# Scores of the forgetting attention as three fp32r products with stacked high and low parts

## What is computed

```python
q = heads(q_in) * (dh ** -0.5)
k, v = heads(k_in), heads(v_in)
logf = jax.nn.log_sigmoid(f_pre.astype(f32)).transpose(0, 2, 1)
F = jnp.cumsum(logf, axis=-1)
...
    s = jnp.einsum('bhtd,bhsd->bhts', qb, k) + (fb[..., None] - F[:, :, None, :])
    s = jnp.where(pb[:, None] >= pos[None, :], s, -jnp.inf)
    p = jax.nn.softmax(s, axis=-1)
    return jnp.einsum('bhts,bhsd->bhtd', p, v)
```

## Time and profile before

| | us |
|---|---|
| median of three runs | 872.34 |
| lowest, highest | 872.18, 875.2 |
| the profiled execution | 872.08 |
| its span, first to last instruction | 870.3 |
| mean granted TensorE clock, share of full speed | 0.995 |
| input projection with the mixers in it, about | 38 to 399 |

### The profile page before, as it was taken

One profiled execution on the slowest core, in us unless ns is written; L12 is line 12 of the kernel. 1 busy time (PEld: TensorE's weight loads), 2 busy tenths in 40 slices (PEclk: granted clock), 3 DMA queues, 4 the chain that ended last, 5 costly groups with the idle time before them and its releaser, 6 DMA issues.

```text
span 870.3 us, 10546 instructions
## 1 busy us (share of the span) xinstructions
PE 847.0 (97%) x3932; PEld 681.4 (78%) x3932; DVE 438.8 (50%) x703; ACT 323.8 (37%) x478; POOL 48.2 (6%) x75
## 2 busy tenths in 40 slices
PE   5999999999999999999999999999999999999996
PEld 3578888877787777787888778888888888888886
DVE  6789877247778654225873453333333333323222
ACT  4535445442323444343333553333333332222231
POOL 5310000000000000000001110000000000000110
PEclk9899999999999999999999999999999999999999
DMA  9833223348775121114234223333333333333322
GB/s 357 264 77 104 72 73 90 79 145 289 253 256 170 49 73 49 49 49 169 74 97 121 73 73 96 96 96 96 96 96 96 96 96 91 105 96 90 103 72 96
DMA packets 149372, 100.67 MB, mean 116 GB/s; under 512 B 11072, under 2 KB 142552, under 8 KB 148312
## 3 DMA queue, kind: packets, MB, share of 16 engines
q1 hardware_dynamic: 149128, 100.14, 37.9%
q10 hardware_dynamic: 208, 0.05, 0.0%
HBM read 97.03 MB, written 2.10 MB: 114 GB/s over the span
## 4 chain that ended last, share of the span: by engine, by line
PE 87%; DVE 5%; DMA 3%; ACT 2%; issue 1%; SPq 1%; DVEq 0%; ACTq 0%
PE bank L1696 25%; PE bank L1698 25%; PE bank L1697 25%; DMA raw<-in_w_in 3%; PE bank L1913 2%; PE bank L1843 1%; PE bank L1935 1%; PE bank L1863 1%; PE bank L1874 1%; DVE wlo L1190 1%; PE bank L1960 1%; ACT whi L696 1%; PE bank L1926 1%; PE bank L1911 1%; PE bank L1815 0%
## 5 line engine op out<-in xcount | busy, mean ns | idle before, releaser
L1696 PE MATMUL bank<-h_lo,whi 128*128 128x512 f32 x712 | 285.9, 402 | 1.8 <-DVE wlo L1190 1.0
L1698 PE MATMUL bank<-h_hi,wlo 128*128 128x512 f32 x712 | 278.1, 391 | 0.0
L1697 PE MATMUL bank<-h_hi,whi 128*128 128x512 f32 x712 | 277.9, 390 | 0.0
L1696 PEld LDWEIGHTS bank<-h_lo,whi 128*128 128x128 f32 x712 | 134.2, 189 | 32.2 <-issue 3.7
L1697 PEld LDWEIGHTS bank<-h_hi,whi 128*128 128x128 f32 x712 | 134.3, 189 | 28.7 <-issue 1.7
L1698 PEld LDWEIGHTS bank<-h_hi,wlo 128*128 128x128 f32 x712 | 134.1, 188 | 28.8
L1190 DVE TENSOR_TENSOR wlo<-raw,whi 128x1024 fp32r<-128x1024 f32 x60 | 73.3, 1223 | 104.7 <-ACT whi L696 104.7
L696 ACT ACTIVATE whi<-raw 128x1024 fp32r<-128x1024 f32 x60 | 63.2, 1055 | 151.3 <-PE bank L1698 107.8
L1698 PE MATMUL bank<-a_hi,wlo 128*128 128x512 f32 x176 | 68.5, 389 | 0.0
L1696 PE MATMUL bank<-a_lo,whi 128*128 128x512 f32 x176 | 68.5, 389 | 0.0
L1697 PE MATMUL bank<-a_hi,whi 128*128 128x512 f32 x176 | 68.5, 389 | 0.0
(11 more groups left out here) (334 smaller groups left out, 1005.8 us busy)
## 6 DMA issues: line engine op xcount, KB each, us to landing
raw<-in_ffn_w SPq DMA_DIRECT2D x60, 512.0 KB, 3.8
raw<-in_w_in SPq DMA_DIRECT2D x44, 512.0 KB, 4.0
slab<-in_mod_w SPq DMA_DIRECT2D x32, 512.0 KB, 5.9
modA<-in_mod_w SPq DMA_DIRECT2D x4, 1024.0 KB, 10.9
modB<-in_mod_w SPq DMA_DIRECT2D x4, 1024.0 KB, 18.4
raw<-in_w_out SPq DMA_DIRECT2D x8, 512.0 KB, 3.7
raw<-in_ffn_w SPq DMA_DIRECT2D x8, 384.0 KB, 3.2
xtok<-in_x SPq DMA_DIRECT2D x4, 512.0 KB, 5.6
```

The costliest lines, as they stand in the source:

```text
L1696: mm(dst, w_h, m_l, start=first, stop=False)
L1697: mm(dst, w_h, m_h, start=False, stop=False)
L1698: return mm(dst, w_l, m_h, start=False, stop=last)
```

## The change

- fq chunks: one activation brings 128 rows into vtmp; ACT copies the two heads' halves into qst as fp32r (q high), and DVE subtracts them into the other half of the same head's 128 rows (fox_q_lo): a head's qst has q high in its own 64 rows and q low in the other 64.
- fk chunks: kf stays. ACT copies it in bodies 30 to 32 into khi, where each head has 128 rows with k high twice (four copies of 64 rows a chunk, fox_k_hi); DVE subtracts to klo, which lies on kf, in place (two a chunk, fox_k_lo).
- fox_scores: three fp32r products: the forget rows with nft and sel widened by zeros to 128 rows; qst by khi over 128 rows; qst's own 64 rows by klo. The product of the low parts is left out.
- POOL's clearing of qpad goes, w_glu is loaded in SP's step 22 behind a wait for the conv's output in place of the start, and hm, ym_lo, yf_hi, fox, mt1 and wglu have other addresses.

```diff
-        hm = at("hm", [P, 3, L], F32, 119)
+        khi = [at("khi0", [P, 3, L], F32R, 119), at("khi1", [P, 3, L], F32R, 131)]
...
-        qpad = at("qpad", [P, FH, L], F32, Z + 18.125)
+        qst = at("qst", [P, FH, L], F32R, Z + 18.125)
         kf = at("kf", [P, 3, L], F32, Z + 30.125)
+        klo = at("klo", [P, 3, L], F32R, Z + 30.125)
...
+                if s == 22:
+                    sp_.wait_ge(s_cx, 3)
+                    sp_.dma_start(wglu[:], w_glu.rearrange("(k p) n -> p k n", p=P)).then_inc(s_wglu, 16)
...
                 elif kind == "fq":
-                    act.wait_ge(s_pad, 3)
-                    A(qpad[0:FD, 2 * i, :], src[0:FD, :], ACT.Identity, bias=bq8[0:FD, i:i + 1],
-                      scale=FD ** -0.5)
-                    A(qpad[FD:P, 2 * i + 1, :], src[FD:P, :], ACT.Identity,
-                      bias=bq8[FD:P, i:i + 1], scale=FD ** -0.5).then_inc(s_evac, 1)
+                    act.wait_ge(s_vt, 6)
+                    if i == 2:
+                        act.wait_ge(s_qlo, 1)
+                    q = vtmp[:, i % 2]
+                    A(q, src[:], ACT.Identity, bias=bq8[:, i:i + 1], scale=FD ** -0.5).then_inc(s_evac, 1)
+                    act.wait_ge(s_evac, s + 1)
+                    A(qst[0:FD, 2 * i], q[0:FD], ACT.Copy)
+                    A(qst[FD:P, 2 * i + 1], q[FD:P], ACT.Copy).then_inc(s_qhi, 1)
...
+            def fox_k_hi(i):
+
+                act.wait_ge(s_mqk, MH)
+                act.wait_ge(s_evac, A_CHUNKS.index(("fk", i)) + 1)
+                even, odd = (khi[h // 3][:, h % 3] for h in (2 * i, 2 * i + 1))
+                A(even[0:FD], kf[0:FD, i], ACT.Copy)
+                A(odd[FD:P], kf[FD:P, i], ACT.Copy)
+                A(even[FD:P], kf[0:FD, i], ACT.Copy)
+                A(odd[0:FD], kf[FD:P, i], ACT.Copy).then_inc(s_khi, 1)
...
+                if 30 <= t < 33:
+                    fox_k_hi(t - 30)
...
+            def fox_q_lo(i):
+
+                dve.wait_ge(s_qhi, i + 1)
+                q = vtmp[:, i % 2]
+                V.tensor_tensor(qst[FD:P, 2 * i], q[0:FD], qst[0:FD, 2 * i].bitcast(F32), ALU.subtract)
+                V.tensor_tensor(qst[0:FD, 2 * i + 1], q[FD:P], qst[FD:P, 2 * i + 1].bitcast(F32),
+                                ALU.subtract).then_inc(s_qlo, 1)
+
+            def fox_k_lo(i):
+
+                dve.wait_ge(s_khi, i + 1)
+                even, odd = (khi[h // 3][:, h % 3] for h in (2 * i, 2 * i + 1))
+                V.tensor_tensor(klo[0:FD, i], kf[0:FD, i], even[0:FD].bitcast(F32), ALU.subtract)
+                V.tensor_tensor(klo[FD:P, i], kf[FD:P, i], odd[FD:P].bitcast(F32), ALU.subtract).then_inc(s_klo, 1)
...
+                if 19 <= t < 22:
+                    fox_q_lo(t - 19)
+                if 30 <= t < 33:
+                    fox_k_lo(t - 30)
...
                     pe.wait_ge(s_mp, NT * MH)
-                    pe.wait_ge(s_evac, A_CHUNKS.index(("fk", 2)) + 1)
+                    pe.wait_ge(s_qlo, 3)
+                if t == 0:
+                    pe.wait_ge(s_klo, h // 2 + 1)
                 b = ps[3 + n % 2][:, 0:ln]
-                mm(b, sel[0:42, MH + h:MH + h + 1].broadcast_to([42, P]), nft[:, t % 2, 0:ln],
+                mm(b, sel[:, MH + h:MH + h + 1].broadcast_to([P, P]), nft[:, t % 2, 0:ln],
                    start=True, stop=False)
-                mm(b, qpad[:, h, t * P:(t + 1) * P], kf[:, h // 2, 0:ln], start=False,
-                   stop=True).then_inc(s_fs, 1)
+                own, q = slice(FD * (h % 2), FD * (h % 2) + FD), qst[:, h, t * P:(t + 1) * P]
+                mm(b, q, khi[h // 3][:, h % 3, 0:ln], start=False, stop=False)
+                mm(b, q[own], klo[own, h // 2, 0:ln], start=False, stop=True).then_inc(s_fs, 1)
```

More of the change, by code:

```diff
@@ L179, in build @@
         wqk = at("wqk", [P, 12, MD], F32, X)
-        wglu = at("wglu", [P, 2, S5W], F32, X + 4.5)
+        wglu = at("wglu", [P, 2, S5W], F32, X + 11.5)
         pm = at("pm", [P, 1280], F32, X + 6.5)
@@ L195, in build @@
         msq = at("msq", [P, NT, MW], F32, Z)
+        hm = at("hm", [P, 3, L], F32, Z)
         mo = at("mo", [P, 3, L], F32, Z + 6.125)
         vf = at("vf", [P, NT, FW], F32, Z + 12.125)
-        qpad = at("qpad", [P, FH, L], F32, Z + 18.125)
+        qst = at("qst", [P, FH, L], F32R, Z + 18.125)
         kf = at("kf", [P, 3, L], F32, Z + 30.125)
+        klo = at("klo", [P, 3, L], F32R, Z + 30.125)
         fz = at("fz", [36, L], F32, Z + 30.125)
@@ L209, in build @@
         bbar = at("bbar", [P, 2, NS5, GD], F32, Z + 39.125)
-        nft = at("nft", [42, 2, L], F32R, Z + 40.125)
+        nft = at("nft", [P, 2, L], F32R, Z + 40.125)
         negr = at("negr", [36, L], F32R, Z + 42.125)
@@ L220, in build @@
         assert Z + 46.125 <= 207.5
-        fox = at("fox", [P, 3, L], F32, X)
-        ym_lo = at("ym_lo", [P, 3, L], F32R, X + 6)
+        fox = at("fox", [P, 3, L], F32, X + 6)
+        ym_lo = at("ym_lo", [P, 3, L], F32R, Z)
         ys_hi = at("ys_hi", [P, 2, L], F32R, X + 13.5)
         ys_lo = at("ys_lo", [P, 2, L], F32R, X + 17.5)
-        yf_hi = at("yf_hi", [P, 3, L], F32R, Z)
+        yf_hi = at("yf_hi", [P, 3, L], F32R, X)
         yf_lo = at("yf_lo", [P, 3, L], F32R, Z + 6)
@@ L233, in build @@
         xT = at("xT", [P, KB, L], F32, XT + 16)
-        mt = [at("mt0", [P, 3, L], F32, 115), at("mt1", [P, 3, L], F32, X)]
+        mt = [at("mt0", [P, 3, L], F32, 115), at("mt1", [P, 3, L], F32, X + 6)]
         sq = at("sq", [P, 2, L], F32, 115)
@@ L292, in build @@
         s_evac = sem("w_in_chunk_out")
+        s_wglu = sem("w_glu_loaded")
+        s_qhi = sem("fox_q_hi")
+        s_qlo = sem("fox_q_lo")
+        s_khi = sem("fox_k_hi")
+        s_klo = sem("fox_k_lo")
         s_scal = sem("s5_scalar_inputs")
@@ L470, in _ @@
             sp_.dma_start(raw[:, 3], win_cols(*A_CHUNKS[3])).then_inc(w_loaded[3], 16)
-            sp_.dma_start(wglu[:], w_glu.rearrange("(k p) n -> p k n", p=P)).then_inc(s_small, 16)
             sp_.wait_ge(s_pad, 1)
@@ L611, in _ @@
             nc.gpsimd.memset(vm[:, :, :, MD], 1.0).then_inc(s_pad, 1)
-            nc.gpsimd.memset(qpad[:], 0.0).then_inc(s_pad, 1)
             for h in range(MH):
@@ L703, in evac @@
                 if kind == "f":
-                    act.wait_ge(s_small, 16 * 16)
+                    act.wait_ge(s_small, 16 * 15)
                     A(fz[:], src[0:36, :], ACT.Identity, bias=fbias[0:36, 0:1]).then_inc(s_evac, 1)
@@ L1295, in m_rows @@
                 link(V.tensor_tensor(negr[32:36, :], negm[:], negr[0:MH, :].bitcast(F32), ALU.subtract))
-                link(V.tensor_scalar(sel[0:42, :], ones[0:42, 0:1].broadcast_to([42, 10]), 0.0, None, ALU.mult))
+                link(V.tensor_scalar(sel[:], ones[:, 0:1].broadcast_to([P, 10]), 0.0, None, ALU.mult))
                 link(V.tensor_copy(sel[0:10, :], ident[0:10, 0:10]))
@@ L1325, in m_args @@
                     dve.wait_ge(s_mnum, h)
+                else:
+                    dve.wait_ge(s_qlo, 3)
                 for j in range(NT):
@@ L1377, in nft_row @@
                     dve.wait_ge(s_ms, NT * MH)
-                    link(V.tensor_scalar(nft[:], ones[0:42, 0:2].unsqueeze(2).broadcast_to([42, 2, L]), 0.0, None,
+                    link(V.tensor_scalar(nft[:], ones[:, 0:2].unsqueeze(2).broadcast_to([P, 2, L]), 0.0, None,
                                          ALU.mult))
@@ L1829, in m_qk @@
                 pe.wait_ge(s_cx, 3)
-                pe.wait_ge(s_small, 16 * 16)
+                pe.wait_ge(s_small, 16 * 15)
                 if h:
@@ L1878, in glu @@
             def glu(n):
+                pe.wait_ge(s_wglu, 16)
                 pe.wait_ge(s_y5l, 16 * 16)
```

## The result

| | before | changed |
|---|---|---|
| median, us | 874.08 | 880.23 |
| lowest to highest, 20 executions each, us | 871.62 to 878.54 | 877.11 to 885.92 |
| ratio, 95% interval | | 1.0076 [1.0058, 1.0094] |
| the profiled execution, us | 872.08 | 877.83 |
| its span, us, and mean granted TensorE clock | 870.3, 0.995 | 876.0, 0.987 |

The forecast was 870.0 us, range 865.5 to 874.5. It was wrong: the change costs 6 us where 2.4 were to be gained, and the range didn't hold the time. The forecast started from before's median of three executions, 872.34; over twenty it is 874.08, which is 1.7 of the 10.2 us between 870.0 and 880.23.

The account below looks back on a forecast made before the run. PE, busy 97% of the span, was taken to bound the kernel. Score products -5.9 us and a new PE wait +3.5 gave -2.4 us, from a median of 872.34 to 870.0 us, range 865.5 to 874.5.

Parts of the forecast that it names:

- The bound (PE): Whole kernel: PE, busy 97% of the span, bounds it; a microsecond of PE work removed is gained unless a wait replaces it.
- the new wait: Ahead of the first score product: PE waits 3.5 us for DVE's weighting of head 3, delayed by the third k chunk's parts.
- The prediction's other bound: Third k chunk: if no record overlaps the next, 4.3 us of slide on DVE and 3.9 us of PE wait.
- rival C: At PE's new wait: 3.5 us idle drops its clock to 1.2 GHz, losing 3.4 us, 873.3 in all; chance 0.15.
- The score products: 24 heads, six at each width: three fp32r products with full-row forget rows gain 0.06 to 0.42 us a head, 5.9 in all.
- The switch of 0.2 at each end: Score products: each change between a product on part of the rows and one on all rows costs PE 0.2 us.
- All of it is PE time in the stretch where PE bounds: Score products: the whole 5.9 us saved was counted as a gain in kernel time.
- Rival A: Ahead of the first score product: no new wait, since DVE or ACT is 3.5 us further on; 866.4 us, chance 0.10.
- Rival B: Score products: the 64-row product brings no switch, three full-rate products a head gain 14.3 us; 861.5 us, chance 0.10.
- Rival D: q and k parts: copies crossing partition halves run at half speed, the third chunk's wait grows 1.3 us; 871.3, chance 0.10.
- q in parts, the w_glu load and the moved tiles at 0: q parts at 144 to 170 us cost 0, at worst 0.5 us; load and tiles 0, at most 0.5 either way.

Follow-up runs that it names:

- e3: The changed kernel with each head's third score product read over all 128 rows where it was 64: 873.01 us, ratio to before 0.9989.
- e4: The kernel before with the third k chunk's four copies and two subtractions added at the change's places, into unused space: 883.69 us, ratio 1.0092.
- the first experiment: The changed kernel with the third k chunk's copies and subtractions one body later (33 in place of 32) on ACT and DVE: 871.3 us, ratio to before 0.9961.

## Why the prediction was wrong

- **The bound (PE), the place and the cause of the new wait: right.** DVE's idle 2.88 us, forecast 2.7; PE's 3.93, forecast 3.5. The term was short by 0.4: four copies take 2.55 us (260.22 to 262.77), not 2.2, and two subtractions 1.42 (262.78 to 264.20), not 1.2. The overlap of 0.1 us was read off other pairs; these copies follow each other at 0.63 and these subtractions at 0.70, without overlap. The prediction's other bound, a slide of 4.3 us and a wait of 3.9, had that; the slide was 4.5.
- **The clock, rival C at 0.15: the step that failed.** It had mechanism and place right and was priced at 3.4; at the wait it cost 2.2 to 2.4 (1.7 us of clock in e3 and e4). The sum had it at nothing. The chance was wrong. What spoke for the fall, an idle stretch of 3.5 us, was itself part of the forecast; against it stood only a wait of 1.01 us, which is no evidence about one of 3.5. It belonged in the forecast.
- **Not foreseen at all: the later falls,** 3.4 us of clock and 2.1 of time in the profiled execution (0.987), and more in eight of the twenty (0.978 or 0.98, 883 to 886 us). No rival had a fall without idle time. In the changed kernel the third k chunk's place brings most of them too, since with it moved no execution is below 0.991; but e3, with the same wait, has none below 0.990. What brings them is open.
- **The score products: prices near right, the gain too large.** Predicted 5.9 us, measured 2.8 with the third k chunk later (medians; 2.2 by spans, at most 5.1 by the interval). The switch of 0.2 at each end held, and one pair at 512 columns went from 2.96 to 2.24 us, 0.72 gained against 0.84. The step that failed here is "All of it is PE time in the stretch where PE bounds". From 262 us on, PE's waits for ACT grew from 2.7 to 4.9 us, 2.2 of the missing 3. Measured from the twelfth main product ahead of a pair to the twelfth behind it, the three pairs of each width gained 0.0, 0.4, 0.9 and 1.4 us by rising width, where 0.4, 1.2, 1.8 and 2.5 were forecast. Two pairs of the twelve, those followed by output transposes, gained nothing: the time went into their wait for ACT's pt. At two pairs of 256 columns and two of 384, 0.9 us went into the wait for the bank. What took the 0.3 us at 128 columns isn't shown.
- **Rival A** was run as the first experiment: 871.3, where 866.4 stood; the 5 us between are the products' missing 3.1 and 1.7 from the higher median of before. **Rival B** is refuted by the 0.43 of L1962 and its successor. **Rival D**: the crossing copies (L772, L773) take 0.63 as the others do.
- **q in parts, the w_glu load and the moved tiles at 0: not isolated.** With the third chunk later the first score product starts at 267.90, before's at 268.04, so nothing ahead of it costs over 0.1 us.

Of the sum: wait 3.9 and products -2.8 would have made +1.1 us, too little to tell from no change. The clock made it 6. Against the forecast of -2.4 the change came out 8.5 us worse: 0.4 from the wait, 3.1 from the products, 5.0 from the clock.

## What to carry to other kernels

Put work that two engines must do in turn where the engine that bounds isn't waiting for what stands behind it; one body later here was worth 8.9 us. A forecast wait on TensorE as long as this one (3.9 us) should be priced with the lower clock behind it, some 2 us at the wait here, and compared over many executions, since the clock differs between executions of one kernel. To price a stretch at low clock, compare the starts of the same product in two traces: where the engine would have waited anyway, it costs less than the clock lost. Look for products on part of the rows (42 and 64 here) among full ones and pad them with zeros before anything is redesigned; then see which wait comes next, because a shorter product only gains up to it.

## What was not expected of the hardware

- A product on 42 or 64 rows among full-row ones costs 0.15 to 0.2 us at its start and as much at its successor's, whatever the width; one on 96 rows costs neither (0.24 and 0.86 us against 0.42 and 1.06).
- The granted clock fell to 0.5 with PE busy in 6.50 of 6.50 us and no idle time ahead, behind one-column and 64-column products and transposes. The Trainium skill, "TensorE: Matmul & The Clock Gate", Why this matters for your kernels, warns of idle gaps between bursts of products; the first fall agrees (3.93 us idle ahead of it), and these rows are a case without a gap.
- That fall is not a property of the program alone. With the same list of instructions, executions of the kernel with eight dummies had 0.993 to 0.994 or 0.984, worth 5 to 6 us of 876. What decides it is open.
